# Groups 14 and 15 with their U turned in advance, fewer up tiles ahead of the picks, later high halves, and compact casts, in a kernel with a product-key retrieval layer

## What is computed

```python
def peer(xn, wq, subkeys, u, v):
    K = PEER_TOPK                                  # 16; 8 heads, N_KEYS 128, 16384 experts, D 1024
    def block(xb):                                 # 128 tokens
        t = xb.shape[0]
        q = (xb @ wq).reshape(t, PEER_HEADS, 2, PEER_DQ // 2)
        s = jnp.einsum('thpd,hpkd->thpk', q, subkeys).astype(jnp.float32)
        s_top, i_top = lax.top_k(s, K)
        cand = (s_top[:, :, 0, :, None] + s_top[:, :, 1, None, :]).reshape(t, PEER_HEADS, K * K)
        c_top, c_idx = lax.top_k(cand, K)
        i1 = jnp.take_along_axis(i_top[:, :, 0], c_idx // K, axis=-1)
        i2 = jnp.take_along_axis(i_top[:, :, 1], c_idx % K, axis=-1)
        e = i1 * N_KEYS + i2
        g = jax.nn.softmax(c_top, axis=-1)
        ue = jnp.take(u, e, axis=0)
        ve = jnp.take(v, e, axis=0)
        act = jax.nn.gelu(jnp.einsum('thkd,td->thk', ue, xb).astype(jnp.float32), approximate=False)
        return jnp.einsum('thk,thkd->td', (g * act).astype(xb.dtype), ve)
    return lax.map(block, xt).reshape(B, T, D)
```

## Time and profile before

| what | value |
|---|---|
| median of 3 runs | 2203.56 us |
| lowest, highest | 2201.19, 2205.31 us |
| the profiled execution's own time | 2197.33 us |
| its span | 2195.5 us |
| granted TensorE clock, mean | 0.982 |
| PE busy | 2077.8 us (95%) |
| PE weight loads | 1147.8 us (52%) |
| DVE busy | 1502.7 us (68%) |
| ACT busy | 827.5 us (38%) |
| POOL busy | 1081.2 us (49%) |
| DMA moved | 514.90 MB, mean 235 GB/s |

### The profile page before, as it was taken

The page is one execution under the profiler, slowest core; times in us unless marked ns, Lnnn a source line. Parts: engine busy times, 40 slices in busy tenths (PEclk is TensorE's granted clock), DMA queues, the critical chain, the costliest instruction groups (busy, mean ns, idle before and its releaser), DMA issues.

```text
span 2195.5 us, 29225 instructions
## 1 busy us (share of the span) xinstructions
PE 2077.8 (95%) x11066; PEld 1147.8 (52%) x11218; DVE 1502.7 (68%) x2689; ACT 827.5 (38%) x1225; POOL 1081.2 (49%) x610
## 2 busy tenths in 40 slices
PE   8999899999989999889999988989999999999998
PEld 4446544444444456445666754545544555555554
...
GB/s 236 0 105 12 154 117 242 258 245 248 254 224 150 66 53 137 252 295 170 329 155 390 379 339 344 307 309 309 311 306 286 306 304 302 307 308 285 317 185 83
DMA packets 277575, 514.90 MB, mean 235 GB/s; under 512 B 131122, under 2 KB 188726, under 8 KB 266436
## 3 DMA queue, kind: packets, MB, share of 16 engines
...
q0 software_dynamic: 36864, 134.23, 17.8%
...
HBM read 416.09 MB, written 67.65 MB: 220 GB/s over the span
## 4 chain that ended last, share of the span: by engine, by line
PE 25%; DVE 13%; DMA 11%; POOL 7%; issue 4%; ACT 1%; ACTq 0%; DVEq 0%; POOLq 0%; SPq 0%
PE ps L2166 8%; DMA arena<-in_peer_u,small 6%; PE ps L2091 6%; PE ps L2118 5%; DMA arena<-in_peer_v,small 4%; PE ps L2154 3%; POOL split L948 3%; POOL arena L937 3%; DVE arena L2829 2%; DVE x_sb L2833 2%; DVE arena L2938 2%; PE ps L2108 1%; DVE arena L2964 1%; DVE arena L2811 1%; PE ps L1787 1%
## 5 line engine op out<-in xcount | busy, mean ns | idle before, releaser
L2166 PE MATMUL ps<-split,arena 128*128 128x512 bf16 x1606 | 371.8, 384 | 4.8 <-DVE arena L2979 1.5
L948 POOL TENSOR_TENSOR split<-ring,split 128x1024 bf16<-128x1024 f32 x128 | 297.1, 2324 | 64.6 <-ACT split L1364 62.8
L2118 PE MATMUL ps<-arena 128*128 128x384 bf16 x1728 | 297.8, 330 | 10.6 <-ACT u_split L1371 9.9
L821 POOL TENSOR_TENSOR split<-ring,split 128x4096 bf16<-128x4096 f32 x26 | 207.2, 7969 | 193.3 <-ACT split L1146 191.0
L1787 PE MATMUL ps<-arena,split 128*128 128x512 bf16 x1316 | 296.5, 380 | 5.9 <-DVE arena L2610 2.0
L937 POOL DMA_INDIRECT arena<-in_peer_u,small x128 | 159.8, 1249 | 257.5 <-DVE arena L2829 240.2
L2166 PEld LDWEIGHTS ps<-split,arena 128*128 128x128 bf16 x1656 | 163.8, 99 | 186.4 <-issue 10.5
L2833 DVE SCALAR_TENSOR_TENSOR x_sb<-arena,small,x_sb 128x1024 f32<-128x1024 f32 x128 | 205.2, 1603 | 71.7 <-DMA arena<-in_peer_v,small 69.9
L2118 PEld LDWEIGHTS ps<-arena 128*128 128x128 bf16 x1728 | 170.4, 99 | 122.4 <-issue 17.5
L2829 DVE SCALAR_TENSOR_TENSOR arena<-arena,bcast 128x1024 f32<-128x1024 f32 x128 | 176.5, 1387 | 80.1 <-DMA arena<-in_peer_u,small 79.5
L1787 PE MATMUL ps<-split,arena 128*128 128x512 bf16 x1034 | 229.6, 381 | 1.2
...
## 6 DMA issues: line engine op xcount, KB each, us to landing
ring<-in_peer_v SPq DMA_DIRECT2D x32, 2048.0 KB, 12.8
ring<-in_peer_u SPq DMA_DIRECT2D x18, 2048.0 KB, 17.1
ring<-in_w_ff SPq DMA_DIRECT2D x16, 2048.0 KB, 8.6
...
ring<-turned_table SPq DMA_DIRECT2D x14, 2048.0 KB, 10.4
gate_matrix<-split SPq DMA_DIRECT2D x12, 2048.0 KB
...
```

Source lines behind the costliest of these rows:

```text
L821: pool.tensor_tensor(split[:, s4 % 2, 1, :], ring[:, (s4 + 5) % RING, :], split[:, s4 % 2, 0, :], ALU.subtract).then_inc(w_lo, 1)
L948: pool.tensor_tensor(split[:, s % 2, 1, at], ring[:, s % 2, at], split[:, s % 2, 0, at], ALU.subtract).then_inc(v_lo, 1)
L2118: mm = pe.matmul(up_bank, a, b, start=n == 0, stop=n == len(terms) - 1)
L2166: mm = pe.matmul(down_bank(t, c), a, w, start=s == 0 and j == 0 and n == 0, stop=s == EX_GROUPS - 1 and j == 3 and n == 2)
```

## The change

It has five parts.

- `PRE` becomes 16: the U of groups 14 and 15 is turned in advance too, four more pairs of row blocks on SP and POOL. The live groups are still 14 to 31, but 14 and 15 are read from the ring as bf16 halves and need no fills. A fill f now belongs to group 16 + f // 8; fills begin with pair i = 1, and all take the raw copy. U of groups 16 and 17 is loaded when the live groups 14 and 15 are through.
- `SELECTED` becomes 30: 29 up tiles run ahead of the picks' turning and one behind it, 24 with the gate steps, 2 after.
- The up tiles of group 14 alternate between banks 7 and 6; the early tiles use four banks throughout.
- The order in the loop: the high and low halves of live sub-tiles 2 and 3 move into the next pair, ACT's copies of fills and of stored high halves stand elsewhere, and DVE's rows stand between other neighbours (16 or 14 a pair as before).
- `top_pairs` and the places are laid out so that the casts write to adjacent places (`[.., heads, 16, 2]` in place of `[.., 2, 16, heads]`), and `pair_keys` compares, multiplies and adds over (head, candidate, pick) in place of (candidate, head and pick).

The same moves are made for groups 28 to 31. The diff, cut (the rest of the loop's order is in the rows behind it):

```diff
-        top_pairs = part(arena, 2048, NT, 2, TOPK, 2 * P_HEADS, dt=BF16)
-        place_pairs = part(arena, 13568, TOPK, 2, dt=BF16)
+        top_pairs = part(arena, 2048, NT, 2 * P_HEADS, TOPK, 2, dt=BF16)
+        places = part(arena, 13568, TOPK, TOPK, dt=BF16)
...
-        SELECTED, GATED, EARLY = 32, 24, 14
+        SELECTED, GATED, EARLY = 30, 24, 14
         LIVE = EX_GROUPS - EARLY
-        PRE = EARLY
+        PRE = 16
...
-        THREE = 48
         def early_bank(m):
-            return bank((6, 7, 4, 5)[m % 4] if m < THREE else (6, 4, 5)[m % 3])[:, 0:TD]
-        up_bank = bank(6)[:, 0:TD]
+            return bank((6, 7, 4, 5)[m % 4])[:, 0:TD]
+        def up_bank(g, j):
+            return bank(7 if g == EARLY and j % 2 else 6)[:, 0:TD]
         turn_to = bank(7).rearrange("p (k e) -> p k e", k=4)
         def fill_place(f):
-            return EARLY + f // 8, f // 2 % 4, f % 2
-        FIRST = 8
+            return PRE + f // 8, f // 2 % 4, f % 2
+        FILLS = 8 * (EX_GROUPS - PRE)
...
-            for p in range(24, 2 * PRE):
-                pre_pair(p, p < 2 * PRE - 1)
+            for p in range(24, 28):
+                pre_pair(p, True)
                 slot_free(p - 24)
                 load_turned(p - 20)
-            for g in (8, 9, 10):
+            pre_pair(28, True)
+            for p, g in ((29, 8), (30, 9), (31, 10)):
+                pre_pair(p, p < 2 * PRE - 1)
                 slot_free(g - RING)
                 load_turned(g)
...
-                    load_u(EARLY)
+                    load_turned(EARLY)
...
-                sp.wait_ge(u_turned, 8 * i + 8)
-                load_u(EARLY + i + 2)
+                if i == 0:
+                    slot_free(EARLY)
+                    load_u(PRE)
+                if i >= 2:
+                    sp.wait_ge(u_turned, 8 * (i - 2) + 8)
+                    load_u(EARLY + i + 2)
...
+                if i == 1:
+                    slot_free(EARLY + 1)
+                    load_u(PRE + 1)
...
             sums(2)
+            pre_late(28)
             sums(3)
+            for p in range(29, 2 * PRE):
+                pre_late(p)
...
-                if f >= FIRST:
-                    if f >= FIRST + 4:
-                        act.wait_ge(u_lo, f - 3)
-                    act.activation(turned_raw[f % 4], turn_to, ACT.Copy).then_inc(u_raw, 1)
+                if f >= 4:
+                    act.wait_ge(u_lo, f - 3)
+                act.activation(turned_raw[f % 4], turn_to, ACT.Copy).then_inc(u_raw, 1)
...
-                g, s, f = EARLY + i, 2 * i, 8 * i + 8
+                g, s, f = EARLY + i, 2 * i, 8 * i - 8
                 if i == EARLY // 2:
                     act.wait_ge(rows_taken, PICKS)
                     act.activation(dots, dots, ACT.Gelu).then_inc(gate_exp, 1)
                 v_high(s, 2)
+                if i > 1:
+                    live_high(g - 1, 2)
                 live_gelu(g, 0)
                 u_high(f)
                 v_high(s, 3)
+                if i > 1:
+                    live_high(g - 1, 3)
                 u_high(f + 1)
-                stored_high(i, 0)
                 v_high(s + 1, 0)
                 live_gelu(g, 1)
+                stored_high(i, 0)
+                u_high(f + 2)
                 stored_high(i, 1)
-                live_high(g, 0)
...
-                if m > THREE:
-                    pe.wait_ge(ex_gelu, m - 2)
-                elif m >= 4:
+                if m >= 4:
...
-                pe.wait_ge(u_lo, 2 * l + 2)
-                pe.wait_ge(ex_gelu, 4 * EARLY + l)
+                if g >= PRE:
+                    pe.wait_ge(u_lo, 8 * (g - PRE) + 2 * j + 2)
+                elif j == 0:
+                    slot, rounds = pre_place(g)
+                    pe.wait_ge(ring_in[slot], arrived(slot, rounds))
+                pe.wait_ge(ex_gelu, 4 * EARLY + (l if l >= 4 else max(l - 1, 0)))
                 terms = up_terms(g, j)
                 for n, (a, b) in enumerate(terms):
-                    mm = pe.matmul(up_bank, a, b, start=n == 0, stop=n == len(terms) - 1)
+                    mm = pe.matmul(up_bank(g, j), a, b, start=n == 0, stop=n == len(terms) - 1)
...
-                own.did(dve.tensor_copy(top_pairs[:, :, n % 2, :, n // 2 * 2:n // 2 * 2 + 2],
+                own.did(dve.tensor_copy(top_pairs[:, :, n % 2 * P_HEADS + n // 2, :, :],
...
-                    own.did(dve.tensor_tensor(match.rearrange("p (c a b) -> p c a b", c=TOPK, b=2),
-                                              half_b[:, key, t, :].rearrange("p (a b) -> p a b", b=2).unsqueeze(1).to_broadcast(by_place),
-                                              places, ALU.is_equal))
+                    own.did(dve.tensor_tensor(match.rearrange("p (h c k) -> p h c k", h=P_HEADS, c=TOPK),
+                                              half_b[:, key, t, :].rearrange("p (h k) -> p h k", h=P_HEADS).unsqueeze(2).to_broadcast(by_place),
+                                              places.unsqueeze(1).to_broadcast(by_place), ALU.is_equal))
...
-                for w in (8 * P, 4 * P, 2 * P):
+                for w in (8 * TOPK, 4 * TOPK, 2 * TOPK):
                     for match in (match0, match1):
-                        own.did(dve.tensor_tensor(match[:, 0:w], match[:, 0:w], match[:, w:2 * w], ALU.add))
+                        m = match.rearrange("p (h r) -> p h r", h=P_HEADS)
+                        own.did(dve.tensor_tensor(m[:, :, 0:w], m[:, :, 0:w], m[:, :, w:2 * w], ALU.add))
...
                 stored_times(i, 3)
                 u_low(f - 1)
+                if i > 1:
+                    live_low(g - 1, 2)
                 rows_taken_to(n + 2, n + 3)
-                live_times(g, 0)
                 u_low(f)
+                if i > 1:
+                    live_low(g - 1, 3)
                 rows_taken_to(n + 3, n + 4)
                 u_low(f + 1)
+                live_times(g, 0)
```

155 lines of the change are left out of this document (61 added, 94 removed).

## The result

The changed kernel takes 2227.09 us (median of 4 runs, 2224.03 to 2230.03), the kernel before 2202.38 us (4 runs): 24.7 us more, a ratio of 1.0117 with an interval of 1.0100 to 1.0135. The forecast was 2211 us, between 2180 and 2234. The profiled execution took 2230.03 us, 32.7 more than that of before.

What follows compares the result with a forecast made beforehand. PE was 95% busy, losing time before and behind the gate stage and in pairs paced by DVE and rows. 21.0 - 3.3 - 2.8 + 0 - 7 = +7.9 on 2197.33, plus 6.2 for the median: 2211 us, range 2180 to 2234.

Steps and rivals of the forecast that it cites:

- my own case: Whole kernel: the summed terms give 2211 us, with 2204 to 2219 as its span; chance 0.45.
- rival C: Ahead of the gate stage and in the loop: late loads, steps of 20.96 us, late U of group 17; 2232 us, chance 0.15.
- The turning of four more pairs: Before the gate stage: DVE waits 21 us for the turning before its one-hots, gate stage starts at 1157.1; +21.0 us.
- rival B: Before the gate stage: turning is quick, steps of 13.69 us; 2193 us, or 2201 if POOL and DVE collide; chance 0.17.
- The two tiles: Before the gate stage: 30 tiles ahead instead of 32; the two are worth nothing there and run behind it.
- No fills in the gate stage: Gate stage: eight fills of 0.41 us each go; -3.3 us.
- the stretch behind it: Behind the gate stage, to pair 1: four fills between down products and 1.3 us of low halves go; -2.8 us.
- The order: Loop, pairs 1 to 6: new order of ACT's and DVE's work booked at 0, between 6 us lost and 36 gained.
- -7 in the pairs 7 to 13: Last seven pairs: the wait of 4.51 us stays, half of the other 13.3 us goes; -7 us.
- The reason that I gave for the 0: First six pairs: DVE waits for rows alone, 61.6 us, so DVE and the rows set the pace, 41 us lost.
- Rival A: First six pairs: the order was the brake, so they fall to near 50.17 us each; 2175 us, chance 0.23.
- The compact casts: Key stage: same 128 elements written, cast still needs the port POOL holds; 0 us, out of 0 to -6.4.

Runs made afterwards that it cites:

- the run with short passes: Changed kernel with three turned-group loads behind the last pair, and POOL's casts and subtractions of the four new pairs cut to 8 columns: 2224.72 us.
- with the loads last: Changed kernel with its loads of turned groups 8, 9 and 10 issued behind the last pair instead of between pairs: 2219.83 us.
- the fastest kernel: Kernel before with new loop order, five row buffers, 14 rows in pairs 1 to 7, 15 in 8 to 13, six put off to last groups: 2142.78 us.

## Why the prediction was right or wrong

The direction was right, and so was the part that makes the loss; the size was short: I had 7.9 us against the profiled execution, the stages show 28.5, the medians 24.7. The turning is within 0.6 us of its forecast. The 20.6 us between 7.9 and 28.5 are the gains that I booked behind it, 13.1 us in all, and small losses that came in their place. The time lies inside the range, above the 2204 to 2219 of my own case and near rival C. As neither of C's two causes came about, it is luck that the range held: its upper end was drawn for C.

**The turning of four more pairs: right.** +21.0 forecast, +20.4 measured, and the turning alone gives +23.3. The steps are as I took them: the one short step, 14.7 us, is that of pair 29, which has no load in front. DVE's wait was taken for 21 us and is 6.30, because what I hid behind it was undersized: I allowed POOL's passes 8 us on the picks, and they cost 15.8. The wait is what is left. The rule of the Trainium skill that I set against the change (SBUF — State Buffer, Who interferes with whom), that a VectorE instruction with two SBUF inputs and a GpSimd one that reads SBUF exclude each other, is borne out by the run with short passes: the picks end 119.0 us behind the first up tile in place of 134.8. In rival B the price of 8 us was wrong for the same reason: with the loads last the picks alone hold the gate stage 15.0 us back.

**The two tiles: right.** PE waited 20.11 us with 29 tiles done; two more (7.8 us) would have been done in that time, and the run of the turning alone, which has them there, waits 13.78.

**No fills in the gate stage, -3.3, and the stretch behind it, -2.8: wrong.** The step that failed is that PE's time was taken for the stage's. The stretch to the first down product grew by 2.7 us; with the fills kept and the turning as late (the turning alone) it is 172.2 us. The five kernels with fills, four buffers and full rows have 172.2 to 173.6, the three without fills 176.3 to 178.6. So the fills had filled time in which PE waits for others. The 2.7 us have two parts. From the start of the gate stage to its last store it took 146.55 us (1160.74 to 1307.29) where it took 145.47 (1136.13 to 1281.60, and the earlier trace rows): +1.1 for -3.3. PE is busy 141.38 us there for 143.17, but it stands 3.59 us for one-hots, before which DVE waited 5.50 us for a U row, and 1.58 for ACT, which waited 4.70 us for a store of the gates. The timelines of PE, DVE and ACT at these places:

```profile
1194.77 0.22 PE L2134 MATMUL ps<-arena 128*128 128x128 bf16 x1 [3.59 <-DVE arena L2951]
...
1188.90 1.23 DVE L2829 SCALAR_TENSOR_TENSOR arena<-arena,bcast 128x1024 f32<-128x1024 f32 x1 [5.50 <-DMA arena<-in_peer_u,small]
...
1264.87 3.78 ACT L1352 ACTIVATE split<-ps 128x1024 f32<-128x1024 f32 x2 [4.70 <-DMA gate_matrix<-split]
```

From the last store to the first down product it took 29.75 us where it took 28.15. At the end of that stretch DVE waits for the gates' transfer, and PE waits 5.56 us behind it:

```profile
1327.10 6.01 DVE L2958 TENSOR_TENSOR arena<-arena 128x384 f32<-128x384 f32 x4 [25.16 <-DMA arena<-gate_matrix]
```

I had named that chain and seen the wait, and booked the gain of the low halves all the same.

From the first down product to pair 1 I had -1.5 us for four fills, and it is +0.5. The fills are gone, but the granted clock is lower there: the first ten products behind the wait start 0.43 us apart, the later ones 0.22. The windows of this stretch, in the columns of the earlier trace rows, of the changed kernel and of the kernel before:

```profile
1337.04:1354.65 17.61, 17.55 (x71) 7.52 (x71) 14.67 (x20) 6.21 (x9) 11.92 (x8) 0.87 1.03 398
```

```profile
1309.75:1326.82 17.07, 17.02 (x87) 8.79 (x88) 17.07 (x25) 9.32 (x16) 9.43 (x7) 1.00 1.03 398
```

Ten products at 0.21 us more each are 2.1 us, which is about what the fills gave. So the longer wait for the stored product was paid twice.

**The order: 0 in the pairs 1 to 6, right in kind** (+3.0, the order alone +2.2). **-7 in the pairs 7 to 13: wrong** (+1.9). The six pairs behind the seventh gave 4.35 us (311.20 to 306.85), and the seventh took 6.2: I said that its wait of 4.51 us stays, and it became 10.49. The order alone does this (11.01 us in that run): row 127 is taken 5.6 us later into the pair. That it is so because more of DVE's work stands ahead of it is my reading, not shown.

**The reason that I gave for the 0 holds only in part.** I argued from DVE's 61.6 us of waits for rows that rows set the pace. More buffers and fewer bytes did bring 10.7 and 19.3 us in those six pairs, so rows do set it. But the waits hardly moved (55.1 and 49.9 us; 41.7 with five buffers and the new order, 36.6 in the fastest kernel), so their sum does not say what the rows cost. And some of the 41 us that I put to DVE and the rows is clock: PE is busy 11.7 us longer in these pairs than in the fastest kernel. Rival A, "the order was the brake", is false with four buffers and worth some 6 us of the loop with five.

**The compact casts, 0: right.** **Rival C: wrong.** The steps are 73.2 us in sum, not 84, and U of group 17 cost PE 0.62 us in pair 2, not 7.

What stays open: whether bandwidth or the round trip of a row is the nearer limit, whether an even spread of the rows would give as much with the old order, and why the turning alone lost 7.7 us in the last seven pairs.
